# A hybrid convolution decoder layer on 8 cores: the stage of the seven-product gates in another order

## The chip, the cores and the metric

One Trainium2 chip, all 8 cores (two dies of four). Each core computes one of eight prompts (2048 tokens) and 16 of the 128 sample sequences (8 tokens each), 2176 tokens in all, with all weights; the cores exchange nothing. The time is device microseconds of the slowest core.

## The reference

```python
u = _rmsnorm(h, g_mix)                                  # (N, T, 1024)
a_b, a_c, a_h, a_z, b_v, b_g, b_z, gate_a, gate_b = jnp.split(u @ w_in, SPLITS, axis=-1)   # 9 x 1024
s = a_c * a_h
ya = (a_b * causal_dwconv3(s) * silu(a_z)) @ w_out_a
v = b_v * sigmoid(b_g)
c = causal_dwconv31(v) + b_conv_b
yb = (silu(layernorm(c, ln_g, ln_b)) * silu(b_z)) @ w_out_b
m = sigmoid(gate_a) * ya + sigmoid(gate_b) * yb
h = h + m @ w_o
h = h + sigmoid(_rmsnorm(h, g_ple) @ w_pg) * (p @ w_pe)
return _rmsnorm(h, g_final)                             # and the ends of both convolution inputs
```

## The kernel before

The tokens of a core are done in two blocks, one after the other. Block 0 has N = 1152 tokens in four groups of wb = 288 (U = 2 units of two groups), block 1 has 1024 in two groups of 512 (U = 1). Channels lie on the partitions in chunks of 128 (j = 0 to 7), tokens along the free axis; `uT` is the normalized input, turned.

Every engine has one queue in the order in which the Python emits it. A helper keeps readers and writers of each named buffer and puts a semaphore wait in front of an instruction whose buffer is not free yet, so a name that overlaps another (an alias) waits too. Weights of 128 columns (256 KB in bf16) come into a ring of 14 slots, `ring`, loaded by GpSimd's queue (L407) in the order of use: `pump` issues the next loads as slots are freed (`wfree`). PSUM has 8 banks, handed out as four pairs by `palloc` (from the list `pairs`, in rotation, `pair_ctr`).

A block runs so:

- Projections b_v, b_g (`s2_proj`), the dwconv31 (`s2_conv`, matmuls of 32 columns over shifted copies that go out to HBM, `vd`, `vsd`, and come back to `reg`), and branch A up to its output projection (`s3_chunk`). `s2_sums` adds up the sum (`accs`) and the sum of squares (`accq`) of the convolution's output `cbuf`. `gate_plain(0)` and `(1)` are plain gate projections.
- `ln_stats`: matmuls with ones (L821) give the LayerNorm sums; ScalarE and VectorE (L830 to L841) make the mean and 1/sigma, which go out through HBM (`lnd`) and come back spread over the partitions in the place of `accs` and `accq` (`rstd`, `mrs`).
- The stage that the change is about. Three kinds of work alternate on TensorE. `g_pair` (L1020) computes two gate chunks by seven products instead of eight (a 2x2 scheme over halves of the channels and of the tokens; `us` are sums of `uT`, `g_weights`, L997, makes four differences of weights on VectorE). It works in banks X = 0, C = 1, Y = 2; ScalarE copies between banks (L1031), VectorE adds (L1037), ScalarE takes the gate through a tanh (L1067). At some places it calls `fill()`, which puts in a quarter of a unit, four matmuls, from a list. A unit (L1076) is one chunk and one u: 16 matmuls into one pair of banks. Kind `z`: b_z, ScalarE's Silu (L1101), with the LayerNorm on `cbuf` beside it (VectorE L1104 and L1107, ScalarE's Silu L1109, and the product L1115 one unit later, `pend_fin`). Kinds `a` and `b`: output projections of both branches, with the gate applied in VectorE's evacuation (L1149), and for `b` the sum of both (L1157). `queue` puts units into the list, `rest` works off what is left, with `pairs` = [2, 3] from the first gate pair on.
- In block 0, `pg` scales one row block of `w_pg` by `g_ple` on ScalarE (L551), in from HBM to `reg` (L547) and out to HBM (`wpgd`, L554); eight in all, one after each of several units. Two buffers, each loaded again after its scaling.
- The loop over BORDER (`b` units, with three gate pairs and with loads for what follows), and the output stage over 128-token tiles: `s6_A` (m @ w_o, L1216), `s6_C` (p @ w_pe, L1264, and the per-layer gate, L1272, with `wpgd`), `s6_E`, `s6_D` (residual and last norm), while the tiles of the next block are normalized (`s1_stats`, `s1_scale`) and turned by DMA (`s1_xbar`).

A unit's matmuls wait for the reader of their bank, as in these lines:

```python
b = palloc()                                              # o_part: a pair of banks
yield from halves(t_, src, ..., u, b)                     # 16 matmuls in four quarters
S.add("dve", ... o = (o + 1) * pp(b), reads=pres(b) + r)  # L1149 reads both banks
```

## Time and profile before

| | us |
|---|---|
| median of 3 runs (lowest, highest) | 889.52 (888.61, 894.49) |
| profiled execution | 891.01 |
| its span on the slowest core (of 882.3 to 889.5) | 889.5 |
| TensorE busy, 5706 matmuls | 838.1 (94%) |
| VectorE busy | 530.4 (60%) |
| ScalarE busy | 331.0 (37%) |
| GpSimd busy | 212.3 (24%) |

The profiled execution is 1.5 us above the median and its time is 1.5 us more than its span. TensorE's waits are what can be won; the granted clock of TensorE has two levels, 1.2 and 2.4 GHz, and stands as 0.5 and 1.0 in the rows, a mean over the stretch. Block 0's stage of gates runs from about 248 to 416 us, its output stage to 494, block 1's from 688 to 817.

### The profile page before, as it was taken

The numbers are of one execution on the slowest core, as the hardware profiler recorded it, in microseconds if no ns is written. First come the engines' busy times: TensorE is split into PE (matmuls) and PEld (weight loads), VectorE is DVE, ScalarE is ACT, GpSimd is POOL, SyncE is SP. The second block draws the span as 40 slices with busy tenths as digits, with TensorE's granted clock in tenths as the row PEclk, the third lists the DMA queues.
The fourth block names the chain that finished last, engine by engine and source line by source line (L and its number), as shares of the span: only waits on it lengthen the run. The fifth ranks groups of instructions, "written<-read, shape, count | busy, mean of one in ns | idle before, by whom it ended". The sixth has DMA issues, their size and how long they took to land.

```text
span 889.5 us, 16897 instructions; the slowest of 8 cores (882.3 to 889.5 us)
## 1 busy us (share of the span) xinstructions
PE 838.1 (94%) x5706; PEld 491.4 (55%) x5706; DVE 530.4 (60%) x782; ACT 331.0 (37%) x523; POOL 212.3 (24%) x402
## 2 busy tenths in 40 slices
PE   7899999999898599999899999999998899999995
PEld 3677777777566477766434444444443344444442
DVE  3545567687754556546667434555668477455566
ACT  4212233233356464231666312222224345331554
POOL 3532223233110121011344222222221122110112
PEclk9999999999899889999999999999999999999998
DMA  8999999999967946769998499999999567775533
GB/s 237 161 176 179 197 171 162 172 159 160 153 137 164 195 81 99 135 112 186 229 254 207 120 154 144 146 141 139 140 146 124 108 102 114 120 157 154 142 109 113
DMA packets 91133, 135.56 MB, mean 152 GB/s; under 512 B 37528, under 2 KB 45992, under 8 KB 89000
## 3 DMA queue, kind: packets, MB, share of 16 engines
q0 software_dynamic: 33392, 57.72, 43.1%
q1 hardware_dynamic: 57512, 76.50, 40.0%
q8 instruction: 47, 0.77, 0.4%
q14 instruction: 38, 0.31, 0.1%
q10 hardware_dynamic: 144, 0.26, 0.1%
HBM read 169.26 MB, written 19.35 MB: 212 GB/s over the span
## 4 chain that ended last, share of the span: by engine, by line
PE 71%; DMA 9%; DVE 9%; issue 5%; ACT 3%; SPq 1%; POOL 1%; DVEq 0%; POOLq 0%; ACTq 0%
PE ps L621 36%; PE ps L1076 13%; PE ps L1020 9%; PE ps L1272 5%; PE ps L1216 4%; PE ps L759 3%; DMA t_reg<-w_pg 3%; DMA t_reg<-wpgd 2%; DMA t_xs<-x 2%; DMA t_reg<-vsd 1%; PE ps L1264 1%; DVE t_tmp L1104 1%; DMA t_ring<-w_in 1%; DVE t_cbuf L1115 1%; DMA vd<-t_vt 1%
## 5 line engine op out<-in xcount | busy, mean ns | idle before, releaser
L621 PE MATMUL ps<-t_uT,t_ring 128*128 128x288 bf16 (+1 forms) x2400 | 374.0, 317 | 3.5 <-DVE t_uT L598 2.3
L621 PEld LDWEIGHTS ps<-t_uT,t_ring 128*128 128x128 bf16 x2400 | 233.2, 98 | 141.2 <-issue 9.1
L407 POOL DMA_DIRECT2D t_ring<-w_in x144 | 78.9, 549 | 280.4 <-PE ps L621 185.8
L1076 PE MATMUL ps<-t_uT,t_ring 128*128 128x288 bf16 (+1 forms) x384 | 65.3, 325 | 9.7 <-ACT t_tmp L1101 9.7
L1272 PE MATMUL ps<-t_reg,t_mis 128*128 128x512 bf16 x272 | 63.3, 386 | 4.9 <-DMA t_reg<-wpgd 2.3
L1076 PE MATMUL ps<-t_yaT,t_ring 128*128 128x288 bf16 (+1 forms) x384 | 65.7, 317 | 0.0
L1076 PE MATMUL ps<-t_cbuf,t_ring 128*128 128x288 bf16 (+1 forms) x384 | 64.4, 317 | 0.0
L1216 PE MATMUL ps<-t_cbuf,t_yaT 128*128 128x512 bf16 x272 | 61.2, 379 | 0.0
L946 DVE TENSOR_TENSOR t_tmp<-ps,t_tmp 128x576 f32<-128x576 f32 (+1 forms) x24 | 21.8, 912 | 60.1 <-PE ps L621 60.1
L1076 PEld LDWEIGHTS ps<-t_uT,t_ring 128*128 128x128 bf16 x384 | 38.5, 100 | 32.5 <-issue 10.0
L683 DVE SCALAR_TENSOR_TENSOR t_vt<-t_tmp,ps 128x512 bf16<-128x512 f32 (+1 forms) x24 | 20.7, 863 | 56.2 <-ACT t_tmp L680 40.7
L441 ACT ACTIVATE t_tmp<-t_cbuf 128x1024 bf16<-128x1024 f32 x37 | 38.8, 1049 | 39.0 <-DVE t_cbuf L1297 37.6
L680 ACT ACTIVATE t_tmp<-ps 128x576 f32<-128x576 f32 (+1 forms) x24 | 18.6, 775 | 91.5 <-PE ps L621 91.5
L1076 PEld LDWEIGHTS ps<-t_yaT,t_ring 128*128 128x128 bf16 x384 | 37.4, 98 | 22.3 <-issue 1.4
L1076 PEld LDWEIGHTS ps<-t_cbuf,t_ring 128*128 128x128 bf16 x384 | 37.6, 98 | 21.4
L1272 PEld LDWEIGHTS ps<-t_reg,t_mis 128*128 128x128 bf16 x272 | 26.8, 99 | 39.1 <-issue 9.6
L444 POOL TENSOR_SCALAR t_msq<-t_ssq 128x1 f32<-128x1 f32 x50 | 16.3, 327 | 134.1 <-ACT t_tmp L441 133.6
L944 ACT ACTIVATE t_tmp<-ps 128x576 f32<-128x576 f32 (+1 forms) x24 | 18.6, 776 | 68.9 <-PE ps L621 68.9
L1216 PEld LDWEIGHTS ps<-t_cbuf,t_yaT 128*128 128x128 bf16 x272 | 26.6, 98 | 31.9 <-issue 0.2
L1031 ACT ACTIVATE ps<-ps 128x288 f32<-128x288 f32 (+1 forms) x42 | 19.2, 457 | 62.4 <-PE ps L1020 61.3
L1149 DVE SCALAR_TENSOR_TENSOR t_tmp<-t_tmp,ps 128x576 f32<-128x576 f32 (+1 forms) x27 | 24.6, 910 | 28.0 <-PE ps L1076 28.0
L932 ACT ACTIVATE t_tmp<-ps 128x576 f32<-128x576 f32 (+1 forms) x24 | 18.6, 776 | 58.7 <-PE ps L621 49.8
(148 smaller groups left out, 1128.9 us busy)
## 6 DMA issues: line engine op xcount, KB each, us to landing
t_ring<-w_in POOLq DMA_DIRECT2D x144, 256.0 KB, 7.8
t_xs<-x SPq DMA_DIRECT2D x30, 512.0 KB, 6.5
y<-t_cbuf SPq DMA_DIRECT2D x16, 512.0 KB, 3.6
t_reg<-vd SPq DMA_DIRECT2D x32, 132.0 KB, 5.8
t_reg<-vd SPq DMA_DIRECT2D x32, 131.9 KB, 6.6
t_reg<-vd SPq DMA_DIRECT2D x32, 131.9 KB, 7.7
t_reg<-vd SPq DMA_DIRECT2D x32, 131.9 KB, 8.6
t_ring<-w_cv POOLq DMA_DIRECT2D x16, 256.0 KB, 9.5
```

What stands on the lines that cost most here:

```text
L407: S.add("pool", lambda e, k=k, src=src: e.dma_start(out=ring[k][:, :], in_=src), writes=[f"ring{k}"], dma=f"ring{k}")
L441: S.add("act", lambda e, c=c: e.activation(out=junk.rearrange("p (h m) -> p h m", h=2), in_=src_ap, func=AF.Square, accum_out=ssq[:, c:c + ...
L621: S.add("pe", lambda e, k=k, si=si, c0=c0: e.matmul(ps[:, b + si, 0:wb], lhsT=ring[k_][:, 128 * k:128 * k + 128], rhs=src[:, k, c0:c0 + wb ...
L683: S.add("dve", lambda e, bv=bv, tg=tg, u=u: e.scalar_tensor_tensor(out=pph(vt[v], u), in0=pcols(two(tg)), scalar=1.0, in1=pcols(pp(bv)), o ...
L759: S.add("pe", lambda e, b=b, r=r, i=i, g=g, wc=wc, rhs=src[:, c0:c0 + w], w=w: e.matmul(ps[32 * g:32 * g + 32, b + r, 0:w], lhsT=ring[kc][ ...
L946: S.add("dve", lambda e: e.tensor_tensor(out=two(tz), in0=pp(bb), in1=two(tz), op=ALU.mult), reads=pres(bb) + [tzr], writes=[tzr])
L1020: S.add("pe", lambda e, k=k: e.matmul(pt(b), lhsT=w[:, 128 * k:128 * k + 128], rhs=src(k), start=first and k == 0, stop=k == 3, skip_group ...
L1031: S.add("act", lambda e: e.activation(out=out, in_=pt(b), func=AF.Copy), reads=[f"ps{b}"], writes=w)
L1076: S.add("pe", lambda e, k=k, si=si, c0=c0: e.matmul(ps[:, b + si, 0:wb], lhsT=ring[k_][:, 128 * k:128 * k + 128], rhs=src[:, k, c0:c0 + wb ...
L1149: S.add("dve", lambda e: e.scalar_tensor_tensor(out=dst.rearrange("p (s n) -> p s n", s=2), in0=two(o), scalar=1.0, in1=pp(b), op0=ALU.add ...
L1216: S.add("pe", lambda e, h=h, k=k: e.matmul(ps[:, b + h, :], lhsT=yaT[:, k, 128 * ti:128 * ti + 128], rhs=wo_t[:, k, 512 * h:512 * h + 512] ...
L1272: S.add("pe", lambda e, h=h, k=k: e.matmul(ps[:, bg + h, :], lhsT=u2Ts[sl][:, k, :], rhs=wpg_t[:, k, 512 * h:512 * h + 512], start=(k == 0 ...
```

## The change

- Order: `gate_plain(1)` moves ahead of the last convolution chunk. Gate pairs now take whole units with them (two in block 0, one in block 1), because `g_pair` calls `fill()` once more at the end of each sub-block; the z and a units between the pairs are fewer and in another order. Units of the `b` loop that are not in a gate pair run by themselves.
- Banks: `gates` uses pairs 2, 3 and then leaves [2, 3, 0, 1]; `run_parts` restricts its last part to pair 3.
- The LayerNorm of `cbuf` is done in place: `z_norm` (two VectorE instructions) two units ahead, `z_silu` one unit ahead. A z unit takes only one temporary. The load of `w_o` goes behind the product.
- Weight scaling in block 0: two at a time at four places, and the loads go to `gfin` and a temporary; `gfin` is loaded late, at i = 7. Without the old buffers row block 7 of `wpgd` can be loaded at i = 1.
- `g_weights` of BORDER[2] and [3] moves into the last run of parts before the `b` gates.
- L841 moves from VectorE to GpSimd.
- Block boundary: the ring's loads are held from i = 2 on in block 0 and let go two per tile of the output stage; `gmix` goes to a temporary at i = 3; the first next tile is normalized at i = 6, with its sums written into `xn`. The order of the x tiles (`XU`) is changed to match.

```diff
+            def pg_tile(t):
+                pgs_tile.append(t)
+                pgs.append((t[0][:, 0:D], t[1]))
...
-                    S.add("dve", lambda e: e.tensor_tensor(out=ts[:, w:2 * w], in0=tm, in1=ts[:, 0:w], op=ALU.mult),
+                    S.add("pool", lambda e: e.tensor_tensor(out=ts[:, w:2 * w], in0=tm, in1=ts[:, 0:w], op=ALU.mult),
...
                         evac(*th(ga, 1, s), pt(C), [f"ps{C}"])
+                        fill()
...
+                def z_norm(i):
+                    if i < len(zs):
+                        j, u = zs[i]
+                        c, r = rng(cbuf[:, j], u), cres(j, u)
+                        S.add("dve", lambda e: e.tensor_tensor(out=c, in0=c, in1=rng(accs, u), op=ALU.mult),
+                              reads=r + [f"rstd{u}"], writes=r)
+                        S.add("dve", lambda e: e.tensor_tensor(out=c, in0=c, in1=rng(accq, u), op=ALU.add),
+                              reads=r + [f"mrs{u}"], writes=r)
+
+                def z_silu(i):
+                    if i < len(zs):
+                        j, u = zs[i]
+                        c, r = rng(cbuf[:, j], u), cres(j, u)
+                        S.add("act", lambda e: e.activation(out=c, in_=c, func=AF.Silu,
+                                                            scale=vcol(V_LNG, j), bias=vcol(V_LNB, j)),
+                              reads=r + ["vecs"], writes=r)
+
                 def z_part(j, u):
+                    i = zs.index((j, u))
+                    z_norm(i + 2)
+                    z_silu(i + 1)
+                    flush(pend_fin)
                     if u == 0:
                         held["z", j] = wuse("in", j, 6)
                     t_ = held["z", j]
@@ -1090,34 +1126,21 @@
                     yield from halves(t_, uT, u_res, u, b)
                     if u == U - 1:
                         wfree(t_)
-                    s4_unit(j, u, b)
-                    if u == U - 1:
-                        last_weights("wo", [j])
+                    tl = tget()
+                    tb, tbr = tu(tl, 0)
+                    S.add("act", lambda e: e.activation(out=two(tb), in_=pp(b), func=AF.Silu),
+                          reads=pres(b), writes=tbr)
+
+                    def fin():
+                        S.add("dve", lambda e: e.tensor_tensor(out=rng(cbufb[:, j], u), in0=rng(cbuf[:, j], u), in1=tb,
+                                                               op=ALU.mult),
+                              reads=cres(j, u) + tbr, writes=[f"yb{j}"])
+                        tput(tl)
+                        if u == U - 1:
+                            last_weights("wo", [j])
+
+                    pend_fin.append(fin)
...
+                def use_pairs(*p):
+                    pairs[:] = p
+                    pair_ctr[0] = 0
+
+                def run_parts(*parts):
+                    for i, p in enumerate(parts):
+                        if i == len(parts) - 1:
+                            use_pairs(3)
+                        if p[0] == "do":
+                            p[1]()
+                        else:
+                            queue(p)
+                            rest()
+
+                def gates(br, c0, ja, jb, *parts):
+                    queue(*parts)
+                    use_pairs(2, 3)
+                    tg[br, ja], tg[br, jb] = g_pair(c0, ja, jb, ev_gate, step)
+                    rest()
+                    use_pairs(2, 3, 0, 1)
...
                 gate_plain(0)
                 flush(pend_sums)
+                use_pairs(*((2, 0) if U == 2 else (0, )))
+                gate_plain(1)
+                use_pairs(1, 2, 3)
                 s2_conv(7)
                 flush(pend_sums)
-                gate_plain(1)
                 g_weights(7, 2, 3)
                 pgk = []
 
                 def pg():
-                    if pgk:
-                        pg_mul(pgk.pop(0))
+                    for _ in range(2):
+                        if pgk:
+                            pg_mul(pgk.pop(0))
 
                 if not bi:
+                    pg_tile(pool.pop())
                     pg_in(0)
                     pg_in(1)
                     pgk.extend(range(NCH))
@@ -1472,77 +1514,83 @@
                     step()
                 ln_stats()
...
                 rest()
-                queue(("a", 1))
-                gates("a", 7, 2, 3)
+                gates("a", 7, 2, 3, ("a", 1))
                 g_weights(7, 4, 5)
-                rest()
-                for p in (("z", 0, 0), ("a", 2, 0), ("z", 0, 1), ("z", 1, 0), ("a", 2, 1)):
-                    queue(p)
-                    rest()
-                    if p[2] == 0:
-                        pg()
-                queue(*((("z", 1, 1), ("z", 2, 0)) if U == 2 else (("z", 2, 0), )))
-                gates("a", 7, 4, 5)
                 pg()
-                rest()
+                z_norm(0)
+                z_norm(1)
+                z_silu(0)
+                if U == 2:
+                    run_parts(("z", 0), ("a", 2, 0), ("z", 1), ("a", 2, 1))
+                else:
+                    run_parts(("z", 0), ("a", 2), ("z", 1))
+                gates("a", 7, 4, 5, ("a", 3))
                 g_weights(7, 6, 7)
-                for p in (("a", 3, 0), ("z", 2, 1), ("z", 3, 0), ("a", 3, 1), ("z", 3, 1), ("z", 4, 0), ("z", 4, 1)):
-                    queue(p)
-                    rest()
-                    if p != ("z", 2, 1):
-                        pg()
-                while pgk:
-                    pg()
-                queue(("a", 4, 0), ("z", 5, 0)) if U == 2 else queue(("a", 4))
-                gates("a", 7, 6, 7)
+                pg()
+                if U == 2:
+                    run_parts(("z", 2), ("a", 4, 0), ("z", 3))
+                else:
+                    run_parts(("z", 2), ("z", 3))
+                gates("a", 7, 6, 7, *((("a", 4, 1), ("z", 4, 0)) if U == 2 else (("a", 4), )))
                 g_weights(8, BORDER[0], BORDER[1])
-                rest()
-                queue(*((("a", 4, 1), ("z", 5, 1)) if U == 2 else (("z", 5), )), ("z", 6), ("z", 7))
-                rest()
+                pg()
+                diff = ("do", lambda: g_weights(8, BORDER[2], BORDER[3]))
+                if U == 2:
+                    run_parts(("z", 4, 1), ("a", 7, 0), ("z", 5), ("do", pg), ("z", 6, 0), diff, ("z", 6, 1), ("a", 7, 1))
+                else:
+                    run_parts(("z", 4), ("z", 5), ("a", 7), diff, ("z", 6))
+                if not bi:
+                    pool.append(pgs_tile[0])
                 pst["ext"] = False
                 pool[:] = [t for t in pool if not t[2]]
-                queue(("a", 5))
-                gates("b", 8, BORDER[0], BORDER[1])
+                gates("b", 8, BORDER[0], BORDER[1], ("z", 7))
                 flush(pend_fin)
-                g_weights(8, BORDER[2], BORDER[3])
-                queue(("a", 6), ("a", 7))
-                rest()
+                run_parts(("a", 5), ("a", 6))
                 pre = {}
                 xst["cap"] = len(XU) if last else XB
                 for i, j in enumerate(BORDER):
-                    queue(("b", j))
                     if i in (0, 2, 4):
+                        gates("b", 8, BORDER[i + 2], BORDER[i + 3], ("b", j))
                         if i < 4:
                             g_weights(8, BORDER[i + 4], BORDER[i + 5])
-                        gates("b", 8, BORDER[i + 2], BORDER[i + 3])
-                    rest()
-                    if i in (0, 4):
-                        xload((XB if last else 0) + 2 + i // 2)
+                    else:
+                        run_parts(("b", j))
+                        if i > 4:
+                            use_pairs(0, 1, 2, 3)
+                    if i in (0, 5):
+                        xload((XB if last else 0) + 2 + 2 * (i // 4))
                     if i == 1:
                         last_weights("wpe", [0, 1])
+                        wpg_load(7)
...
+                        wst["hold"] = not last
+                    if i == 3 and nxt:
+                        gm = [t for t in pool if f"tmp{hf}_{TW // hf - 2}" not in t[1]][0]
+                        pool.remove(gm)
+                        gmx.update(ap=gm[0][:, 0:D], res=gm[1])
+                        S.add("sp", lambda e: e.dma_start(out=gmx["ap"], in_=gmix_d), writes=gm[1], dma="gmix")
+                    for k in {3: (0, 1), 4: (2, 3), 5: (4, 5, 6)}.get(i, ()):
                         wpg_load(k)
+                    if i == 6 and nxt:
+                        s1_scale(*s1_stats(nxt[0], (xn[0], "xn0")), 0)
+                    if i == 7 and nxt:
+                        pre[1] = s1_stats(nxt[1], (xn[1], "xn1"))
+                        S.add("sp", lambda e: e.dma_start(out=gfin[:], in_=gfin_d), writes=["gfin"], dma="gfin")
...
+                    if nxt:
+                        wst["hold"] = False
+                        pump(2)
```

## Rows read from the trace of the kernel before

**Rows 1.** Busy time by stretch: start:end, us, each engine (x instructions), clock, DMA share, GB/s
```profile
247.60:311.50 63.90, 50.80 (x404) 38.20 (x402) 33.44 (x57) 33.99 (x58) 7.93 (x15) 0.93 0.79 157
...
360.30:409.00 48.70, 44.81 (x360) 34.40 (x358) 25.25 (x44) 16.65 (x42) 8.70 (x16) 1.00 0.68 125
...
452.50:494.00 41.50, 41.22 (x189) 18.50 (x190) 28.82 (x25) 25.27 (x38) 16.26 (x26) 0.96 0.87 214
```

**Rows 2.** Waits of TensorE: its line, releaser: us in total, times, longest
```profile
PE ps L1076 <- ACT t_tmp L1101: 9.7, 1, 9.7
PE ps L1020 <- ACT ps L1031: 6.3, 7, 2.3
PE ps L1020 <- DVE ps L1037: 3.9, 5, 1.4
...
PE ps L759 <- DMA t_reg<-vsd: 3.8, 1, 3.8
...
PE ps L1272 <- DMA t_reg<-wpgd: 2.3, 1, 2.3
PE ps L1272 <- DVE t_cbuf L1227: 2.1, 1, 2.1
```

**Rows 3.** Timeline (start, us, engine, line, [idle before]): issue, scaling and TensorE
```profile
293.48 0.62 SPq L547 DMA_DIRECT2D t_reg<-w_pg  x1
...
309.65 1.15 ACT L551 ACTIVATE t_xs<-t_reg,t_vecs 128x1024 bf16<-128x1024 f32 x1 [3.99 <-DMA t_reg<-w_pg]
...
311.48 4.00 PE L1076 MATMUL ps<-t_uT,t_ring 128*128 128x288 bf16 x16 [9.71 <-ACT t_tmp L1101]
```

**Rows 4.** Timeline: the run of b units at the end of block 0's loop
```profile
403.52 12.90 PE L1076 MATMUL ps<-t_cbuf,t_ring 128*128 128x288 bf16 x104
...
406.73 0.75 DVE L1149 SCALAR_TENSOR_TENSOR t_tmp<-t_tmp,ps 128x576 f32<-128x576 f32 x1 [0.34 <-PE ps L1076]
```

**Rows 5.** Timeline: from VectorE's end to TensorE's start
```profile
385.24 0.46 DVE L1037 TENSOR_TENSOR ps<-ps,t_tmp 128x288 f32<-128x288 f32 x1
...
385.85 0.41 PE L1020 MATMUL ps<-t_xs,t_ring 128*128 128x288 bf16 x2 [0.78 <-DVE ps L1037]
```

**Rows 6.** Timeline: sums, table load and the first gate pair, block 0
```profile
247.97 0.75 DVE L810 TENSOR_TENSOR t_accq<-t_accq,t_tmp 128x576 f32<-128x576 f32 x1
...
252.24 1.28 ACT L837 ACT_TABLE_LOAD   x1 [0.71 <-DVE t_tmp L834]
...
255.05 0.65 PE L1020 MATMUL ps<-t_mis,t_vt 128*128 128x288 bf16 x4 [0.54 <-ACT ps L1031]
```

**Rows 7.** Timeline: the same place in block 1
```profile
690.47 1.22 DVE L1149 SCALAR_TENSOR_TENSOR t_reg<-t_xs,ps 128x1024 f32<-128x1024 f32 x1
...
691.95 1.86 PE L1020 MATMUL ps<-t_uT,t_ring 128*128 128x512 bf16 x4 [3.81 <-DVE t_reg L1149]
...
696.11 1.03 PE L1020 MATMUL ps<-t_mis,t_vt 128*128 128x512 bf16 x4
```

**Rows 8.** Timeline: L1104 of successive z units, 2.20 us apart, in block 1 3.60
```profile
334.75 0.75 DVE L1104 TENSOR_TENSOR t_xs<-t_cbuf,t_accs 128x576 f32<-128x576 f32 x1
...
336.95 0.75 DVE L1104 TENSOR_TENSOR t_tmp<-t_cbuf,t_accs 128x576 f32<-128x576 f32 x1
...
728.32 1.22 DVE L1104 TENSOR_TENSOR t_tmp<-t_cbuf,t_accs 128x1024 f32<-128x1024 f32 x1
...
731.92 1.22 DVE L1104 TENSOR_TENSOR t_tmp<-t_cbuf,t_accs 128x1024 f32<-128x1024 f32 x1
```

**Rows 9.** By line: weight differences (ns min/median/max); GpSimd's longest kind (us, mean ns)
```profile
L997 DVE TENSOR_TENSOR t_vt<-t_ring,t_vt x28: 415/422/426, 249.2 to 788.2; 128x512 bf16<-128x512 bf16 x28
...
L719 POOL TENSOR_SCALAR t_vt<-t_vt 128x480 bf16<-128x480 bf16 x8 | 12.7, 1594 | 4.4 <-DMA t_vt<-sb 4.4
```

**Rows 10.** DMA: the w_pg loads after 262 us (median us to landing); queue 0 in all
```profile
t_reg<-w_pg SPq DMA_DIRECT2D x6, 512.0 KB, 7.3
...
q0 software_dynamic: 33392, 57.72, 43.1%
```

More of the change, by code:

```diff
@@ L266, in build_program @@
         XT0 = 2 * HMAX
-        pgs = [reg[:, 4 * NTB + D * i:4 * NTB + D * (i + 1)] for i in range(2)]
         pgo = [t[:, 12 * HMAX:12 * HMAX + D] for t in (xsa.bitcast(BF16), mis)]
@@ L395, in wsrc @@
                     {"oa": w_oa, "ob": w_ob, "cv": w_cv}[nm][j, :, :]
-            wst = dict(nl=0, nd=0, done=set())
+            wst = dict(nl=0, nd=0, done=set(), hold=False)
             def pump(maxn=4):
@@ L426, in wfree @@
                     wst["nd"] += 1
-                pump()
+                if not wst["hold"]:
+                    pump()
             def wdone(n=1):
@@ L471, in go @@
                 nxt = tiles_of(b + 1) if b + 1 < len(BLOCKS) else []
-                XU.extend(own[0:2] + nxt[0:3])
-                for i in range(2, len(own)):
+                XU.extend(nxt[0:2])
+                for i in range(len(own)):
                     XU.append(own[i])
-                    XU.extend(nxt[i + 1:i + 2])
+                    XU.extend(nxt[i + 1:i + 2] if i else [])
             XB = len(XU) - len(tiles_of(1))
@@ L1433, in do_block @@
                     pair_ctr[0] = 0
-                    S.add("sp", lambda e: e.dma_start(out=gfin[:], in_=gfin_d), writes=["gfin"], dma="gfin")
                 else:
@@ L1531, in do_block @@
                             out=hist_d[:, 0:480], in_=sb_d.rearrange("c s w -> c (s w)")), dma="hist")
-                    if i == 5 and nxt:
-                        S.add("sp", lambda e: e.dma_start(out=gmix, in_=gmix_d), writes=["gmix"], dma="gmix")
                     if i == 5 and last:
                         S.add("pool", lambda e: e.drain())
-                pairs[:] = [0, 1, 2, 3]
+                if nxt:
+                    s1_xbar(0, 0)
                 s6_Aev(0, *s6_A(0))
```

64 lines of the change are left out of this document (21 added, 43 removed).

## The prediction

> **What bounds it now.** Read the busy time by stage first: TensorE is the limit everywhere and short of work in few places. In the first gate stage (`a` and `z` units, block 0) it worked 50.8 of 63.9 us at a granted clock of 0.93; the stage with the `b` units lost 3.9 of 48.7 us [rows 1]. Then the waits of TensorE: one of 9.7 us behind a Silu (L1101), 6.3 us behind ScalarE's copies (L1031), 3.9 us behind VectorE's addition (L1037), 3.8 us for `vsd`, 2.3 + 2.1 us in the output stage [rows 2], and 3.8 us behind the evacuation of a unit in block 1 [rows 7]. Last, what holds the releasers. The Silu stood behind a weight scaling (L551) at 309.65 whose `w_pg` load was issued at 293.48, 16 us earlier [rows 3].
>
> **The sum.** It is made against the profiled execution (889.5 us span, 891.0 us in all); the median shown is 889.5, so the answer is lowered by 1.5.
>
> *Weight scaling in four groups of two.* The loads go to `gfin` and a temporary, and two of them have a whole gate pair plus units (some 20 us) until they are read, twice over. The 9.7 us go. Of the 6.3 us behind L1031, about 1 follows the LayerNorm chain and stays; 5.3 go (a scaling in front of it, or the chain of normalization and Silu that is now done a unit ahead). Clock: behind such stalls TensorE ran at 1.2 GHz instead of 2.4. Sixteen matmuls took 4.00 us [rows 3] in place of 2.0 (0.124 each [rows 4]), a group of four in block 1 1.86 in place of 1.03, and the next one too, 1.6 us in all [rows 7]. I count 2.3 us behind the long stall and 1.5 behind a shorter one of L1031. **Gain 18.8.** The fourth group has only units z4.1, a7.0, z5 (7.8 us) between its load's issue and its read; landing took 7.3 us in the median, 16 at worst [rows 3, 10]. Two scalings, two Silus and two evacuations then stand in ScalarE's queue ahead of the evacuation for which a7.1 waits: 1.9 us of stall if the load is in time, 1.8 more at 8 us (0 to 8). **Cost 3.7.**
>
> *Fourth fill in the gate pair.* A `b` unit's evacuation no longer lands between L1037 and its reader: **gain 3.9**. One z-normalization now falls inside a pair: 0.6 lost. Where z and a units alternate, VectorE needs 2.2 us per z unit (block 1: 3.6) against 1.96 (3.46) on TensorE [rows 8], with four weight differences of about 0.42 us before [rows 9] and two normalizations in advance: 1.1 us lost in block 0 after the first group.
>
> *Order around conv 7, L841 on GpSimd, pairs 1 to 3 there.* Block 0: gate 1 (two units, 3.9 us) fills the 3.8 us wait for `vsd`; then conv 7 is followed by only one unit (1.96) before the LayerNorm sums, whose last addition began at 247.97 [rows 6]. TensorE starts conv 7 as before, when `vsd` lands, but at full clock, so that addition begins about 1.6 us sooner, at 246.4, and ends at 247.1; `accs` is ready 0.7 us before it. TensorE, with conv 7 (64 short matmuls, 2.1 us) and one unit behind the landing at about 239.1, is ready at 243.2 and waits about 3.2 us. What is late next is this sum. From it runs a chain: L834, a table load at 252.24, Ln, Exp, the copy of bank 0, the product at 255.05 [rows 6]. L834 stood 3 us behind the last addition, for a gate unit lay before the sums; now it starts at 248.9, and the product at 252.2: 2.85 us sooner. Block 1: the a-unit's evacuation began at 690.47 because L841 stood in front of it [rows 7]; now neither L841 nor the bank holds TensorE. The sums hold it some 2.5 us (conv 7 comes a unit of 3.46 us later, but VectorE was 1.3 us behind in any case), they end at 686.4, the a-unit's second half at 689.1, two products and a filling quarter take 0.86 each, and the product that ran at 696.11 runs at 691.9: **gain 2.85 + 4.2**. L841 itself on GpSimd: nearest rows 0.42 (one VectorE operand pair) and 1.59 us for 480 columns [rows 9]; I take 1.3. It only delays `rstd`, read 8 us later, so between 0 and 0.3 us; 0.
>
> *Output stage of block 0.* wpg 7 is loaded from i = 1, ring loads are held, the first next tile is normalized before the stage. The 2.3 and 2.1 us and the half clock behind (0.04 of 41.5 = 1.7 us [rows 1]) go: **gain 6.1**. The copies of `gmix` and `gfin` are one 512 KB load each and fall beside 20 us of work: 0 (if late, their 8 to 18 us show in VectorE's first tile).
>
> *One pair of banks.* `run_parts` sets `use_pairs(3)` for its last part, and each b part is a run of its own. In the kernel before, successive units alternate between pairs 2 and 3, so the multiply-add L1149 of one runs under the matmuls of the next: 104 matmuls without a gap in 12.9 us, L1149 about 0.25 us behind each unit's end [rows 4]. With one pair the next unit's first matmul waits for it: 0.25 + 0.75 + 0.15 (L1037 ended 385.70, TensorE went on at 385.85 [rows 5]) = 1.15 us; in block 1, where a unit has 512 columns, 0.25 + 1.22 + 0.25 = 1.7 [rows 7]. No row shows such a unit itself; it cannot gain, and is at most a VectorE cycle more, 3.3. Block 0: i = 1 and 3 two units each, with a weight difference in VectorE's queue 2.5 us; i = 5, 6, 7 six units, 6.9; a6 2.3; z3.1 (ScalarE) 1.0: **cost 15.2**. Block 1 has one unit per part. After a gate pair its unit is in pair 2 and the next part starts in pair 2 too: z0, z2, z4 at 1.7, a5 at 1.45 (Silu); i = 6 and 7 at 1.7; z1 follows a2 in pair 3, and a2's evacuation stands behind three normalizations and a weight difference, 3.35. **Cost 13.3.**
>
> What the rules say: by the Trainium skill (Perfetto Trace Analysis, Matmuls) independent matmul groups should rotate through PSUM banks so that evacuation overlaps the next group. By that rule the units above show their evacuation; the trace agrees in so far as the alternating units show none [rows 4]. By it the sum is as forecast; if the evacuations did not show, it would be A's.
>
> *New stalls over 2 us.* The two before the sums, a7.1 and z1 of block 1: four at 1.6 us of half clock would be 6.4; as two are near 2 us and may be spared, I take **cost 5** (0 to 6.4).
>
> Sum: gains 18.8 + 3.9 + 7.05 + 6.1 = 35.9. Costs 3.7 + 0.6 + 1.1 + 15.2 + 13.3 + 5 = 38.9. Net 3.0 slower: 894.0 as profiled, **892.5 as a median**. A large stall is removed, and many small ones are put in.
>
> **The rivals.**
> A, faster: evacuations don't reach TensorE at full price, for instance because the units' first matmuls meet a bank already free or VectorE starts earlier. For it: in every stretch where pairs alternate VectorE has room (25.3 of 48.7 us busy [rows 1]). Against it: the dependence is in the code, and a write of a bank needs its last reader done. The single pair costs 28.5 above; without the 25 that aren't z1's queue it is 867.5, at half of them 880. Chance 0.22.
> B, slower: TensorE's clock falls in the run of six b units, i = 5 to 7, where it would rest 1.15 us in each 3.1. Six units of 16 matmuls at 1.2 GHz cost 6 × 1.96 = 11.8 more: 904. It decides from the point where the granted clock of that stretch is below 1. Against it: in the stage of the gates five waits of 0.2 to 1.4 us left the clock at 1.00 [rows 1, 2]. The Trainium skill (TensorE: Matmul & The Clock Gate, A second HAM failure mode: psum-queue depth-cycling) tells of such oscillation where PSUM banks make TensorE idle between groups. Chance 0.14.
> C, slower: the held ring loads meet x, y and the transposes in the output stage. By queue 0's row a 256 KB load takes 43.1% of 889.5 us / 57.72 MB = 1.66 us of all 16 DMA engines [rows 10]; of the fourteen held, about eleven are new there, 18 us, where the second half had 0.13 of 41.5 us, 5.4, free [rows 1]: 12 us over, if that share is a capacity: 904. Against it: the share is no fixed amount of bytes, 0.79 went with 157 GB/s in the gate stage and 0.87 with 214 here [rows 1], and nothing needs the ring before block 1. Chance 0.12.
> The rest, 0.52, is the forecast, whose own range is 883 to 903 (loads 0 to 8, the stalls' clock 0 to 7, evacuations ±5).
>
> **Numbers.** A measurement tells about 1% (8.9 us) from nothing. Faster 0.22 is A; slower 0.26 is B and C; within 1% 0.52 the forecast. The range 877 to 904 leaves out the lower half of A and little above: about 0.2.
>
> **What would show it.** Right: no wait of TensorE behind L1101 near the scaling; units at i = 5 to 7 spaced about 3.1 us, not 1.96, each released by VectorE L1149 (about 14 us of such waits in block 0, 8 in block 1); TensorE waits for `accs` before the sums in both blocks; no wait for wpgd. The forecast is wrong if those units are still 1.96 us apart (A), if matmuls among them take double (B), or if the output stage waits for transposes or x (C).

## The result and the profile after

The changed kernel takes **930.96 us** (median of 4 runs, 927.03 to 933.57), the kernel before beside it 890.20 (4 runs, 888.61 to 894.49): ratio **1.045 [1.039, 1.051]**, 40.8 us slower. The forecast was 892.5 with a range to 904. In some runs the cores of one die have a lower granted clock and take longer; the medians and ratios, those below too, leave such runs out. The profiled run took 927.03, its slowest core 925.5 (all: 909.1 to 925.5).

Its lines are numbered a little higher: L630 is the projection (before L621), L768 the convolution (L759), L830 the LayerNorm sums (L821), L1029 the products (L1020), L1040 and L1046 the copy and the addition between banks (L1031, L1037), L1086 the unit (L1076), L1131 the z unit's Silu (L1101), L1153 the tanh of `gate_plain` (L1130), L1172 the gated evacuation (L1149), L1303 and L1311 the output stage's products (L1264, L1272), L599 and L1275 the two transposes (L590, L1236), L561 the weight scaling (L551). In the rows of e11 below, L1308 is this L1311, and in those of e10 L1130 is this L1131.

Waits of TensorE in the changed kernel (line, releaser: us in total, times, longest), to be laid beside [rows 2]:

```profile
PE ps L1086 <- DVE t_tmp L1172: 13.6, 12, 1.6
PE ps L1086 <- ACT t_xs L1131: 13.3, 2, 12.7
PE ps L1311 <- DMA t_mis<-t_mis: 11.6, 2, 11.1
PE ps L1086 <- DVE t_reg L1172: 8.6, 4, 3.3
PE ps L830 <- DVE t_accs L815: 5.8, 2, 3.2
PE ps L1311 <- DVE t_cbuf L1348: 3.9, 1, 3.9
PE ps L630 <- ACT t_xs L1153: 2.8, 2, 1.5
```

The old list is gone nearly whole, and a longer one stands in its place. The longest wait is again a Silu behind a scaling, as in [rows 3]. This is that place in the timeline (start, us, engine, line, what it waited for):

```profile
314.47 0.58 SPq L556 DMA_DIRECT2D t_gfin<-w_pg  x1
315.86 0.60 SPq L556 DMA_DIRECT2D t_tmp<-w_pg  x1
...
326.46 1.15 ACT L561 ACTIVATE t_xs<-t_gfin,t_vecs 128x1024 bf16<-128x1024 f32 x1 [5.67 <-DMA t_gfin<-w_pg]
332.80 1.15 ACT L561 ACTIVATE t_mis<-t_tmp,t_vecs 128x1024 bf16<-128x1024 f32 x1 [5.19 <-DMA t_tmp<-w_pg]
...
336.68 4.00 PE L1086 MATMUL ps<-t_yaT,t_ring 128*128 128x288 bf16 x16 [12.71 <-ACT t_xs L1131]
```

The two loads landed 12 and 17 us after their issue. The fourth scaling group stood on them twice, two Silus of normalized chunks and two evacuations behind it, and TensorE for 12.7 us.

The run of b units, which took 12.9 us for 104 matmuls in [rows 4], as the waits inside it (six alike, two shown) and VectorE's evacuation:

```profile
408.84 2.12 PE L1086 MATMUL ps<-t_cbuf,t_ring 128*128 128x288 bf16 x16 [1.01 <-DVE t_tmp L1172]
411.96 2.12 PE L1086 MATMUL ps<-t_cbuf,t_ring 128*128 128x288 bf16 x16 [1.01 <-DVE t_tmp L1172]
...
414.19 0.76 DVE L1172 SCALAR_TENSOR_TENSOR t_tmp<-t_tmp,ps 128x576 f32<-128x576 f32 x1 [1.51 <-PE ps L1086]
```

A unit every 3.13 us, of which 1.01 is its own evacuation, and every matmul group at full clock (2.12 us for 16).

The output stage of block 0: TensorE, then SyncE's queue (where the duration is how long the queue held the instruction), then GpSimd's ring loads, held until here:

```profile
461.45 5.34 PE L1311 MATMUL ps<-t_reg,t_mis 128*128 128x512 bf16 x16 [11.09 <-DMA t_mis<-t_mis]
482.78 4.92 PE L1311 MATMUL ps<-t_reg,t_mis 128*128 128x512 bf16 x16 [3.90 <-DVE t_cbuf L1348]
...
450.65 2.20 SPq L487 DMA_DIRECT2D t_xs<-x  x2
452.89 9.91 SPq L599 DMA_TRANSPOSE t_uT<-t_mis  x1
463.00 4.99 SPq L1275 DMA_TRANSPOSE t_mis<-t_mis  x1
...
442.55 1.15 POOL L405 DMA_DIRECT2D t_ring<-w_in  x2
451.84 1.14 POOL L405 DMA_DIRECT2D t_ring<-w_in  x2
```

The stretch by busy time (start:end, us, PE, PEld, DVE, ACT, POOL busy, granted clock, DMA share, GB/s), the same view as [rows 1]:

```profile
324.00:340.00 16.00, 3.32 (x15) 2.12 (x16) 3.37 (x6) 4.88 (x6) 0.53 (x1) 0.64 0.64 149
340.00:426.40 86.40, 73.88 (x579) 55.85 (x578) 40.15 (x63) 26.23 (x63) 12.64 (x24) 0.99 0.65 121
447.00:466.80 19.80, 8.71 (x33) 3.42 (x32) 7.17 (x6) 6.02 (x10) 5.12 (x10) 0.74 1.25 156
```

From 447 to 467 TensorE works 8.7 of 19.8 us, and the DMA engines' share is 1.25 with 156 GB/s; before, a share of 0.87 went with 214 GB/s [rows 1].

**Where the time went, by stage.** Each number is the median over the eight cores of the profiled run; a stage is bounded by the first or last matmul of a line (first product of a gate pair, first b unit, first L1303 tile, last L1311 tile). The columns to the right are kernels of the experiments below.

| stage, us | before | after | e1 | e2 | e3 | e4 | e7 | e9 | e11 | e12 |
|---|---|---|---|---|---|---|---|---|---|---|
| to block 0's first product | 253.4 | 253.5 | 253.0 | 253.2 | 253.6 | 254.2 | 253.8 | 251.8 | 253.4 | 251.9 |
| gates of block 0 | 105.0 | 109.1 | 109.3 | 107.3 | 103.1 | 102.4 | 95.5 | 96.8 | 96.9 | 95.9 |
| its b units | 63.2 | 70.5 | 71.2 | 59.7 | 70.5 | 60.0 | 60.0 | 60.0 | 59.7 | 71.1 |
| its output stage | 67.3 | 74.8 | 64.5 | 79.8 | 76.6 | 66.4 | 66.5 | 64.0 | 75.6 | 67.5 |
| to block 1's first product | 198.3 | 198.8 | 198.9 | 198.2 | 199.0 | 198.7 | 198.2 | 194.3 | 194.4 | 194.3 |
| gates of block 1 | 81.3 | 89.5 | 91.9 | 83.4 | 89.4 | 83.3 | 84.6 | 83.6 | 83.6 | 90.0 |
| its b units | 51.5 | 54.9 | 54.9 | 51.4 | 54.9 | 51.4 | 51.4 | 51.4 | 51.4 | 54.9 |

The last stage is 65 us in all. The output stage of block 0 differs most between cores (after: 72.1 to 84.1, and 82.8 on the slowest core, which had 70.1 before), and the time is that of the slowest core, so that its cost in time is above the median's.

### The profile page after: what moved, and what is told of

Its sections match the earlier page's. It is cut to its first block, busy times and chain, and to the rows that moved or that the text cites. A ratio compares the mean times of both kernels' runs of the same rounds, so it can differ in the third digit from the quotient of the medians.

```text
span 925.5 us, 16909 instructions; the slowest of 8 cores (909.1 to 925.5 us)
## 1 busy us (share of the span) xinstructions
PE 841.7 (91%) x5706; PEld 490.7 (53%) x5706; DVE 530.5 (57%) x780; ACT 330.6 (36%) x523; POOL 215.0 (23%) x404
## 4 chain that ended last, share of the span: by engine, by line
PE 77%; DMA 7%; DVE 7%; issue 4%; ACT 3%; SPq 2%; POOL 0%; DVEq 0%; POOLq 0%; ACTq 0%
PE ps L630 37%; PE ps L1086 17%; PE ps L1029 9%; PE ps L1311 5%; PE ps L1255 4%; PE ps L768 3%; DMA t_mis<-t_mis 2%; DMA t_tmp<-w_pg 2%; DMA t_cbuf<-x 2%; DVE t_tmp L1172 1%; PE ps L1303 1%; SPq L599 1%; DMA t_ring<-w_in 1%; DMA t_xs<-x 1%; DVE t_reg L1172 0%
## 5 line engine op out<-in xcount | busy, mean ns | idle before, releaser
L630 PE MATMUL ps<-t_uT,t_ring 128*128 128x288 bf16 (+1 forms) x2400 | 373.1, 317 | 6.1 <-ACT t_xs L1153 2.8
L630 PEld LDWEIGHTS ps<-t_uT,t_ring 128*128 128x128 bf16 x2400 | 232.9, 98 | 143.5 <-issue 11.8
L405 POOL DMA_DIRECT2D t_ring<-w_in x144 | 79.3, 552 | 225.0 <-PE ps L630 189.1
L1086 PE MATMUL ps<-t_yaT,t_ring 128*128 128x288 bf16 (+1 forms) x384 | 70.6, 331 | 16.9 <-ACT t_xs L1131 13.3
L1086 PE MATMUL ps<-t_cbuf,t_ring 128*128 128x288 bf16 (+1 forms) x384 | 66.8, 317 | 13.6 <-DVE t_tmp L1172 13.6
L1311 PE MATMUL ps<-t_reg,t_mis 128*128 128x512 bf16 x272 | 64.5, 392 | 16.1 <-DMA t_mis<-t_mis 11.6
L1086 PE MATMUL ps<-t_uT,t_ring 128*128 128x288 bf16 (+1 forms) x384 | 65.1, 322 | 9.4 <-DVE t_reg L1172 8.6
L1086 PEld LDWEIGHTS ps<-t_yaT,t_ring 128*128 128x128 bf16 x384 | 38.4, 102 | 43.3 <-issue 21.7
L1086 PEld LDWEIGHTS ps<-t_cbuf,t_ring 128*128 128x128 bf16 x384 | 36.7, 98 | 37.8 <-issue 17.3
L444 POOL TENSOR_SCALAR t_msq<-t_ssq 128x1 f32<-128x1 f32 x50 | 14.3, 285 | 179.5 <-ACT t_tmp L441 163.3
L1086 PEld LDWEIGHTS ps<-t_uT,t_ring 128*128 128x128 bf16 x384 | 37.6, 99 | 33.5 <-issue 14.1
L1311 PEld LDWEIGHTS ps<-t_reg,t_mis 128*128 128x128 bf16 x272 | 26.9, 100 | 51.8 <-issue 23.3
L1172 DVE SCALAR_TENSOR_TENSOR t_tmp<-t_tmp,ps 128x576 f32<-128x576 f32 (+1 forms) x27 | 24.5, 909 | 35.3 <-PE ps L1086 35.3
L1040 ACT ACTIVATE ps<-ps 128x288 f32<-128x288 f32 (+1 forms) x42 | 19.3, 460 | 67.1 <-PE ps L1029 66.9
```

The lines of the kernel that those rows point to most:

```text
L405: S.add("pool", lambda e, k=k, src=src: e.dma_start(out=ring[k][:, :], in_=src), writes=[f"ring{k}"], dma=f"ring{k}")
L630: S.add("pe", lambda e, k=k, si=si, c0=c0: e.matmul(ps[:, b + si, 0:wb], lhsT=ring[k_][:, 128 * k:128 * k + 128], rhs=src[:, k, c0:c0 + wb ...
L1040: S.add("act", lambda e: e.activation(out=out, in_=pt(b), func=AF.Copy), reads=[f"ps{b}"], writes=w)
L1086: S.add("pe", lambda e, k=k, si=si, c0=c0: e.matmul(ps[:, b + si, 0:wb], lhsT=ring[k_][:, 128 * k:128 * k + 128], rhs=src[:, k, c0:c0 + wb ...
L1172: S.add("dve", lambda e: e.scalar_tensor_tensor(out=dst.rearrange("p (s n) -> p s n", s=2), in0=two(o), scalar=1.0, in1=pp(b), op0=ALU.add ...
L1311: S.add("pe", lambda e, h=h, k=k: e.matmul(ps[:, bg + h, :], lhsT=u2Ts[sl][:, k, :], rhs=wpg_t[:, k, 512 * h:512 * h + 512], start=(k == 0 ...
```

## The experiments

A time is the median of the runs, a ratio is to the runs of the kernel before on the same chip.

| kernel | us | ratio, 95% |
|---|---|---|
| e1_nohold | 913.7 | 1.026 [1.021, 1.031] |
| e2_pairs | 904.9 | 1.015 [1.011, 1.019] |
| e3_pglate | 924.1 | 1.038 [1.031, 1.046] |
| e4_all | 886.2 | 0.996 [0.993, 0.999] |
| e5_oldconv | 924.0 | 1.037 [1.033, 1.040] |
| e6_conv | 881.0 | 0.988 [0.984, 0.992] |
| e7_split | 877.6 | 0.985 [0.981, 0.989] |
| e8_l841 | 885.9 | 0.994 [0.992, 0.997] |
| e9_best | 872.7 | 0.980 [0.976, 0.983] |
| e10_evfirst | 870.4 | 0.979 [0.975, 0.982] |
| e11_hold | 888.9 | 0.997 [0.994, 1.001] |
| e12_onepair | 895.6 | 1.005 [1.003, 1.007] |
| e13_l841 | 878.2 | 0.984 [0.978, 0.990] |
| e14_noreset | 871.8 | 0.977 [0.975, 0.979] |
| e15_both | 875.4 | 0.982 [0.979, 0.985] |
| e16_before_order | 889.4 | 0.998 [0.996, 1.000] |

### One suspected part undone at a time: e1 to e4

**e1_nohold**, the ring loads not held:

```diff
-                        wst["hold"] = not last
...
-                    if nxt:
-                        wst["hold"] = False
-                        pump(2)
```

> The changed kernel with the ring loads never held in block 0 and not let go two per tile in the output stage; all else as changed. Theory 1 (the held loads of weights, which run beside x loads, y writes and the DMA transposes of the output stage, are what makes TensorE wait 11.1 + 3.9 us there for the turned tile): the output stage of block 0, 90.6 us in the changed kernel against 77.8 before, comes back to about 76 to 79 us, the wait for the transposes to 0 to 3 us, the time from 931 to about 917 (913 to 920). Theory 2 (the new order of the x loads, the late load of gfin and the early first tile are to blame, not the ring): the waits for the transposes stay at 6 to 12 us on most cores and the time within 4 us of 931.

913.7 us, 17 less than the change. The output stage falls from 74.8 to 64.5 us; of the other stages none moves by more than 0.7 us but the gates of block 1, which take 2.4 us more (89.5 to 91.9). The transposes of the u tiles in that stage, by line, in the changed kernel and then in e1 (ns min/median/max in SyncE's queue):

```profile
L599 SPq DMA_TRANSPOSE t_uT<-t_mis x7: 1237/2072/9915, 439.5 to 505.2; - x7
```
```profile
L599 SPq DMA_TRANSPOSE t_uT<-t_mis x7: 1237/1270/2601, 439.4 to 487.5; - x7
```

Without ring loads in flight no transpose of a u tile on this core is held for more than 2.6 us; the other kind, `t_mis`, is held for at most 3.2 (4.4 on any core) and lands in 4.1 instead of 6.3 us in the median.

**e2_pairs**, the bank pairs as before:

```diff
-                        if i == len(parts) - 1:
-                            use_pairs(3)
...
-                    use_pairs(2, 3)
+                    pairs[:] = [2, 3]
...
-                    use_pairs(2, 3, 0, 1)
...
-                        if i > 4:
+                        if i == 7:
                             use_pairs(0, 1, 2, 3)
```

> The changed kernel with the pairs of PSUM banks 2 and 3 in rotation from the first gate pair on, never reset, as in the kernel before. Theory 1 (each unit in a bank pair that was just used waits for its evacuation at full price): the 17 waits behind L1172 (13.6 + 8.6 + 1.1 + 1.0 us on core 1) and the 2.2 us behind L1131 go but for about 3 us behind normalizations in block 1, 22 us in all; 931 becomes about 909 (905 to 913). Theory 2 (VectorE is the real limit between gate pairs and the wait only moves to its next reader, L1046): half of them or more come back behind L1046, 920 to 926.

904.9 us, 26 less. The b units of block 0 run 72 matmuls without a gap again, 8.98 us:

```profile
403.81 8.98 PE L1086 MATMUL ps<-t_cbuf,t_ring 128*128 128x288 bf16 x72
```

The three stages in which units follow each other lose 10.8, 6.1 and 3.5 us; those are the evacuations shown, 20.4 of the 26 us. The output stage, which this edit does not touch directly, grew from 74.8 to 79.8 us in the median; why is open, and in the changed kernel the cores already differ by 12 us there.

**e3_pglate**, the fourth scaling group behind a7.1:

```diff
-run_parts(("z", 4, 1), ("a", 7, 0), ("z", 5), ("do", pg), ("z", 6, 0), diff, ...)
+run_parts(("z", 4, 1), ("a", 7, 0), ("z", 5), ("z", 6, 0), diff, ...)
...
+                pg()
                 if not bi:
                     pool.append(pgs_tile[0])
```

> The changed kernel with the fourth group of weight scalings moved from between z5 and z6 to behind a7.1, just ahead of the b gates. Theory 1 (the wait of 12.7 us is the w_pg load of about 17 us, issued only 7.8 us of matmuls before its reader, in front of the evacuations of z6): a7.1 no longer waits; the load issued at 315.9 still lands at about 333, and ScalarE's copies of the b gate pair, which TensorE reaches at about 326, wait for it: 5 to 7 us in place of 12.7 + 2.3 of half clock, time 931 to about 922 (919 to 925). Theory 2 (the load is slow because TensorE's stall lets other loads pile up, or the other way round, so that moving the reader changes its landing): it lands within 10 us, no stall, 916; or the stall just moves whole, 929 to 931.

924.1 us, 7 less, though the intervals of the two ratios overlap (1.038 [1.031, 1.046] against 1.045 [1.039, 1.051]); clearer is the stage itself, 109.1 to 103.1 us. The predicted wait stands behind the product's copies instead (6.4 us behind L1040 on core 1). So the wait moves with the group: it belongs to the landing of the loads, not to the place.

**e4_all**, all three together.

> All three edits together (ring not held, pairs 2 and 3 in rotation, fourth scaling behind a7.1). Theory 1 (the three costs are separate): 931 - 14 - 22 - 9 = 886 (880 to 892), below or level with the kernel before at 890. Theory 2 (they cover for each other: without the waits for banks the w_pg load is later still against TensorE, and the output stage is reached sooner than its loads): 895 to 905.

886.2 us: 17 + 26 + 7 make 50, and 44.7 came back. That the parts overlap in time is the likely reason; no run shows it. What is left of the change is worth about as much as the old kernel.

### What is left: the order, the last weight, L841, and a better kernel (e5 to e10)

**e6_conv** and **e5_oldconv** put convolution 7 back ahead of `gate_plain(1)`, in e4 and in the change:

```diff
-                use_pairs(*((2, 0) if U == 2 else (0, )))
-                gate_plain(1)
-                use_pairs(1, 2, 3)
                 s2_conv(7)
                 flush(pend_sums)
+                gate_plain(1)
```

> The changed kernel with its three costly parts undone (as in e4_all, 888.4 us), and besides convolution 7 again ahead of gate_plain(1), without the two settings of the pairs round it. Theory 1 (the new order gains nothing in block 0, because the first evacuation of gate_plain stands behind convolution 6's on ScalarE and a unit waits 1.3 to 1.5 us for it, and convolution 7's sums are still awaited for 3.2 us): 885 to 891 us. Rival (the forecast's own term, 2.85 us in block 0 and 4.2 in block 1 gained by the order): undoing it costs 7 us, about 895.

> The changed kernel (930 us) with one part undone: convolution 7 ahead of gate_plain(1) as in the kernel before, and no setting of the pairs there. Theory 1 (in block 1 the order costs 4.4 us: a unit waits 1.4 for L1153, the sums wait 2.6 for accs, and the clock falls behind it; in block 0 two more, which later waits swallow): 922 to 926 us. Rival (the forecast's, by which the order gained 7 us): 937.

881.0 and 924.0 us: 5.3 and 6.9 less. In e5 that is theory 1; in e6 theory 1 fell (no gain from undoing the order), and the rival's sign with it: the forecast had the order bring 7 us, and it costs 5 to 7. In block 1 it costs 4.4 us (198.7 to 194.3).

**e7_split**: weight 6 scaled ahead of b's first pair product, weight 7 behind it.

```diff
-            pgs = [(gfin[:], ["gfin"])]
+            pgs = [None, (gfin[:], ["gfin"])]
...
-                pgs.append((t[0][:, 0:D], t[1]))
+                pgs[0] = (t[0][:, 0:D], t[1])
...
                 if not bi:
+                    pg_mul(pgk.pop(0))
                     pool.append(pgs_tile[0])
...
                 flush(pend_fin)
+                pg()
                 run_parts(("a", 5), ("a", 6))
```

> e4_all with the last group of scaling taken apart: weight 6 is scaled before the first pair product of b, weight 7 only behind that pair product; the two stage tiles change places, so that the one which goes back to the pool holds weight 6. Theory 1 (w_pg 7 lands 17 us after its issue, and ScalarE stood for it 4.9 us with the pair product's copies behind it): the 6.6 us wait of TensorE for L1040 falls to 1 or 2 us, 882 to 884 us. Rival (the scaling is a wait that only moves, because the loads share the DMA engines with the ring's): a wait as long stands at the b unit behind it, 888 us.

877.6 us, 8.6 less than e4, and the gates of block 0 fall from 102.4 to 95.5. ScalarE waits 0.96 us for one load and not at all for the other (e9_best, which has this part):

```profile
329.21 1.15 ACT L561 ACTIVATE t_xs<-t_tmp,t_vecs 128x1024 bf16<-128x1024 f32 x1 [0.96 <-DMA t_tmp<-w_pg]
...
340.99 1.14 ACT L561 ACTIVATE t_mis<-t_gfin,t_vecs 128x1024 bf16<-128x1024 f32 x1
```

**e8_l841** has the product mean times rstd (L841 before) on VectorE in e4, by the one line that e13 shows below.

> e4_all with the mean times rstd of the normalisation (one 288 or 512 wide product per chunk) back on VectorE. Theory 1: the operation is one of a chain that is waited for only at the first normalised chunks, which the statistics reach early; 888 us, within 2. Rival (the forecast's: GpSimd frees VectorE for the evacuations beside it): 891 us or more.

885.9 us against 886.2: no difference that the intervals can tell.

**e9_best** is e6 and e7 in one.

> e7_split and e6_conv together: the likely best version. Theory 1: the gain of e7_split stands (5 to 6 us), the order is worth nothing: 880 to 885 us, faster than the kernel before by 0.5 to 1 per cent. Rival: 889 or more, if the order was worth 7 us.

872.7 us, faster than the kernel before by 2.0% [1.7, 2.4]. The gains of the two add up (5.3 + 8.6 against 13.5 from e4).

**e10_evfirst** takes the z unit's evacuation ahead of the next chunk's Silu:

```diff
                     z_norm(i + 2)
-                    z_silu(i + 1)
                     flush(pend_fin)
...
                           reads=pres(b), writes=tbr)
+                    z_silu(i + 1)
```

> e9_best (872.7 us) with the two ScalarE instructions of a z unit in the other order: the Silu that evacuates its bank pair first, the Silu of the next normalised chunk behind it. Theory 1 (the next unit waits 3.5 us in block 0 and 3.8 in block 1 for L1131, because that one stands behind a Silu which waits for VectorE's second normalisation, itself behind four weight differences; and the half clock behind each stall costs 1.9 and 1.2 more): both waits fall under 1 us, 863 to 867 us. Rival (the product of the chunk comes later and something else waits, the pair's own evacuation or the product on VectorE): 870 to 876.

870.4 us, within the interval of e9. TensorE's waits in e9 and in e10 (core 1):

```profile
PE ps L1086 <- ACT t_tmp L1131: 7.7, 3, 3.8
PE ps L1029 <- ACT ps L1040: 1.0, 2, 0.6
```
```profile
PE ps L1029 <- ACT ps L1040: 4.0, 8, 1.1
PE ps L1086 <- ACT t_tmp L1130: 3.8, 3, 2.0
```

Half of the wait is gone, and three of the 3.9 us are back behind the product's copies, which now find a Silu in front of them. The rival was right.

### One suspected part done alone: e11 and e12

e9_best with the hold of e1 put back, and with the pairs of e2 put back.

> e9_best with one part of the change put back: the ring loads held from the third b unit on and let go two by two in the output stage of block 0. Theory 1 (held loads meet the x loads and the DMA transposes there, and the transposes that the SyncE queue issues are slowed): the output stage of block 0 grows from 64 us (median of the cores) to 74 to 80, 884 to 890 us. Rival (the hold only hurts together with the other parts, whose stalls shift it): under 877.

> e9_best with one part of the change put back: one bank pair for the last part of each run, pairs reset at each gate pair. Theory 1 (evacuation shown, 1.01 us a unit in block 0 and 1.6 in block 1): the stage of the b units of block 0 grows from 60.0 to 70.5 us and those of block 1 by 6 and 3.5, 890 to 896 us. Rival (a part of that was the clock behind other stalls or the order round convolution 7): under 885.

888.9 us (+16.2) and 895.6 us (+22.9). Each shows in its own stages in the main: the hold in the output stage of block 0 (64.0 to 75.6 us), the single pair in the three stages of units (+11.1, +6.4, +3.5). What else moved by more than 1 us is the way to block 0's first product in e11 (+1.6) and the output stage in e12 (+3.5), where these edits do not act directly. The waits of e11 on core 2, and e12's on core 0:

```profile
PE ps L1308 <- DMA t_mis<-t_mis: 17.2, 4, 13.0
```
```profile
PE ps L1086 <- DVE t_tmp L1172: 14.2, 12, 1.6
PE ps L1086 <- DVE t_reg L1172: 6.8, 3, 3.3
```

### Who brought the 4 us ahead of block 1: e13 to e16

With the old order the way to block 1's first product is 194.3 us, against 198.3 before, so something else in the change brings 4.0. Two things differ: L841 is on GpSimd, and the pair counter is set to zero ahead of the output stage, so that block 1 meets its pairs shifted. e13 undoes the first in e10, e14 the second, e15 both; e16 is the kernel before with the new order alone.

```diff
-                    S.add("pool", lambda e: e.tensor_tensor(out=ts[:, w:2 * w], ...
+                    S.add("dve", lambda e: e.tensor_tensor(out=ts[:, w:2 * w], ...
```
```diff
-                            use_pairs(0, 1, 2, 3)
+                            pairs[:] = [0, 1, 2, 3]
```
```diff
+                pairs[:] = [2, 0] if U == 2 else [0]
+                pair_ctr[0] = 0
+                gate_plain(1)
+                pairs[:] = [1, 2, 3]
+                pair_ctr[0] = 0
                 s2_conv(7)
                 flush(pend_sums)
-                gate_plain(1)
```

> e10_evfirst (870.4 us) with the mean times rstd back on VectorE. Theory 1 (part of the 4 us that the front of block 1 gained over the kernel before came from this move: there the a-unit's evacuation began at 690.47, behind it, and TensorE waited 3.8 us for that evacuation): the stretch from the end of block 0's output stage to block 1's first product grows from 194.4 to 196.5 us or more, 872 to 875 us. Rival (the gain came from the bank pairs, which are counted anew ahead of block 1, so that the product meets another pair): no change, 869 to 872.

> e10_evfirst with the pair counter not set to zero ahead of block 0's output stage, as in the kernel before. Theory 1 (with the mean times rstd on GpSimd the a-unit's evacuation is done in time whatever the pair): 194.4 us in that stretch, 869 to 872 us. Rival (the pair is what counts): the wait of the first product for L1172 is back with 2 to 4 us, 872 to 875.

> e13_l841 and e14_noreset together: the two ways in which the front of block 1 differs from the kernel before are both undone. All theories: the stretch is 198 us again, as in the kernel before, 874 to 876 us; if it stays at 194.4, the cause is a third one.

> The kernel before with one part of the change done alone: gate_plain(1) ahead of convolution 7, with the pairs (2, 0) for it and (1, 2, 3) from then on. Theory 1 (the order costs time by itself: 1.4 us behind L1130 and 2.6 us for accs in block 1, a like amount in block 0; but it also meets another pair than the one TensorE waited 3.8 us for in block 1): block 0's first product 1 to 2 us later, block 1's front as before or 1 us worse, 890 to 894 us against some 891. Rival (the forecast: 2.85 and 4.2 us gained): 884.

Medians to block 1's first product: e10 194.4, e13 194.3, e14 196.3, e15 198.3. The times of whole runs (878.2, 871.8 and 875.4 against 870.4) can't part the theories, for the intervals overlap or touch; the stretch and its waits can. TensorE's wait there, in e13, e14 and e15 (core 1):

```profile
671.16 1.02 PE L1086 MATMUL ps<-t_yaT,t_ring 128*128 128x512 bf16 x4 [2.07 <-DVE t_reg L1172]
```
```profile
671.52 1.02 PE L1029 MATMUL ps<-t_uT,t_ring 128*128 128x512 bf16 x4 [1.79 <-DVE t_reg L1172]
```
```profile
673.11 1.87 PE L1029 MATMUL ps<-t_uT,t_ring 128*128 128x512 bf16 x4 [3.80 <-DVE t_reg L1172]
```

The last is the wait of [rows 7] (3.81) with its half clock behind it. Each edit takes about half of it: the shifted pairs let the first product by, so that in e13 a filling quarter waits 2.07 us inside the gate pair instead (gates of block 1: 83.0 against 80.9), and with L841 away the evacuation starts earlier. The theories of e13 and e14 stood against each other, and each held for half. e16, the order alone, is worth nothing to the kernel before: 889.4 us, ratio 0.998 [0.996, 1.000]. Its block 0 reaches the first product 1.8 us later (255.2), block 1 0.9 us earlier (197.4) and has gates of 79.3 instead of 81.3.

## Why the prediction was wrong

By its own steps:

- **Four scaling groups, the gain: right.** 9.71, 2.35 and 1.83 us of waits are gone with about 2.5 us of half clock behind them, 16.4 against 18.8.
- **The fourth group, cost 3.7: wrong.** The step took 8 us for the loads' landing, near the median of 7.3 [rows 10], though its own range of up to 8 us went with a load at 16 [rows 3]. It was 12 and 17 us, the stall 12.71 and the half clock behind it 1.9 (4.00 us for 16 matmuls instead of 2.12): 14.6 in place of 3.7 and 1.6 of clock. Two 512 KB loads issued 1.4 us apart land one after the other; the row of the long one was the nearer. e3 and e7 together took 15 us out.
- **L1037: right.** 3.9 us of such waits became 1.3 (0.29 and 1.00), 2.6 gained against 3.9 less 0.6.
- **Order round convolution 7, gain 7.05: wrong, in sign.** In block 0 the sums' wait came as computed (3.22), but conv 7 began at 241.33 instead of 239.2, because `gate_plain(1)` found its first bank behind the tanh of `gate_plain(0)`, which itself stood behind convolution 6's evacuations (1.29 us), and because TensorE was already 0.7 us later at `gate_plain(0)`; and the half clock behind the sums' wait (3.69 us for 16 matmuls) lay on the way: the product of [rows 6] ran at 255.40, not at 252.2. In block 1 the step gave the order 4.2 us that L841's move and the shifted pairs bring without it (e13 to e15), and did not see that the order then costs 4.4 there: a wait of 1.46 for L1153 and one of 2.62 for `accs`, where the old order has 0.5 to 1.2. Undone, it gives 5 to 7 us back (e5, e6, e9). The four waits in the changed kernel, two of block 0 and two of block 1:

```profile
237.32 4.08 PE L630 MATMUL ps<-t_uT,t_ring 128*128 128x288 bf16 x32 [1.29 <-ACT t_xs L1153]
248.78 0.69 PE L830 MATMUL ps<-t_accs,t_onesf 128*32 128x288 f32 x8 [3.22 <-DVE t_accs L815]
...
701.28 3.61 PE L630 MATMUL ps<-t_uT,t_ring 128*128 128x512 bf16 x16 [1.46 <-ACT t_xs L1153]
711.19 1.08 PE L830 MATMUL ps<-t_accs,t_onesf 128*32 128x256 f32 x8 [2.62 <-DVE t_accs L815]
```

- **Output stage, gain 6.1: wrong, and the largest miss.** It grew by 7.5 us in the median and by 12.7 on the slowest core. Rival C named it: held loads meet x and the transposes. It put 12 us on it and a chance of 0.12; it costs 17 (e1) or 16 (e11). C argued with bytes, and set against itself that nothing needs the ring before block 1. What is late are the transposes: the ring's loads aren't needed, but they slow what is. Without the hold the stage takes 64.5 us, 2.8 less than before.
- **One pair of banks, cost 28.5: right.** The waits are 12.5 us in block 0 (2.1 in the a units, 10.4 in the b units) with 0.9 for z3.1, and 13.0 in block 1, 3.26 of them at z1 (forecast 3.35); time 26.1 (e2) or 22.9 (e12). One unit in block 0 was 1.01 us instead of 1.15.
- **Half clock behind new stalls, 5: a little low.** 1.6 behind the sums of block 0, 1.4 behind those of block 1, 1.7 behind z1, and the 1.9 at a7.1 that is counted above: 6.6. The step expected to be spared some of it; all four stalls had it.

Rival A fell with the 1.01 us rows. Rival B fell too: six rests of 1.01 us, one per 3.13, left every group at 2.12 us, and the stretch at a granted clock of 0.99. The Trainium skill (TensorE: Matmul & The Clock Gate, A second HAM failure mode: psum-queue depth-cycling) tells of another kernel, with 512 columns, whose short idles between groups made the clock swing; here, with 288 columns and rests of 1.01 us, it didn't. The rule of Perfetto Trace Analysis (Matmuls), in the Trainium skill, to rotate independent groups through PSUM banks, holds: 1.01 us per unit of 288 columns and about 1.6 per unit of 512 where it is broken.

The misses in one sum: scaling 9.3, order 7.5 (7.05 expected, 0.5 lost), output stage 18.8 on the slowest core (6.1 expected, 12.7 lost), together 35.6 of the 38.5 us between 892.5 and 931.0.

What stays open: why a w_pg load takes 12 to 17 us there (loads of w_o, `ring` and `wpgd` were in flight with it; none of them was taken away alone), and why in e9 the output stage is 2.5 us shorter than in e7, whose cores differ by 7 us there.

## What to carry to other kernels

Before work is moved into a stage, ask what its loads do to the transfers that the stage waits for, not only when the moved data is needed. Two bank pairs in rotation hide a unit's evacuation, one shows it each time; setting the list anew for each short run of units does the same as having one. And when several edits meet at one wait, price each against the kernel that has the others: here an order worth nothing to the old kernel cost 5 to 7 us in the new one, where other edits had already taken the wait that it was to save.

## What was not expected of the hardware

SyncE's queue was held by single DMA transposes for 9.9, 7.6 and 5.0 us while GpSimd's ring loads and the x loads were in flight, for at most 3.2 on that core in e1 without them, and everything behind in that queue waited with it. The DMA engines' share then stood at 1.25 with 156 GB/s; so a share near 1 says that transfers are in hand, not how many bytes they move. The kernel e9, which holds no loads back, still has one such transpose (7.3 us, core 1), issued while two ring loads and the load of `gfin` were in flight, but before its output stage. Short rests of TensorE left the clock alone (1.01 us in the run of b units; 2.07 us in e13, where four matmuls of 512 columns then took their 1.02 us). A rest of 1.98 us in e10 did not: 16 matmuls took 3.00 us instead of 2.12 behind it, and behind one of 3.51 in e9 they took 4.00, so that near 2 us a stall's clock can't be told in advance:

```profile
269.71 3.00 PE L1086 MATMUL ps<-t_yaT,t_ring 128*128 128x288 bf16 x16 [1.98 <-ACT t_tmp L1130]
```
```profile
271.92 4.00 PE L1086 MATMUL ps<-t_yaT,t_ring 128*128 128x288 bf16 x16 [3.51 <-ACT t_tmp L1131]
```
